# Order of the Hyena back transform, and operand loads of the RWKV scan issued one by one

## What is computed

```
def hyena_mixer(u, conv_w, conv_b, filt, skip):
    ...
    x0, x1, v = jnp.split(uc, 3, axis=-1)
    z = (v * x1).astype(jnp.float32)
    ...
    y = jnp.fft.irfft(jnp.fft.rfft(z, n=2 * L, axis=1) * jnp.fft.rfft(k2, axis=0)[None],
                      n=2 * L, axis=1)[:, :L]
    y = y + z * skip.astype(jnp.float32)
    return (x0.astype(jnp.float32) * y).astype(u.dtype)

def wkv7_scan(r, w, k, v, a, b, reverse):
    def step(S, inp):
        rt, wt, kt, vt, at, bt = inp
        sa = jnp.einsum('bhvk,bhk->bhv', S, at)
        S = S * wt[:, :, None, :] + sa[..., None] * bt[:, :, None, :] + vt[..., None] * kt[:, :, None, :]
        return S, jnp.einsum('bhvk,bhk->bhv', S, rt)
```

## Time and profile before

| | |
|---|---|
| median of 3 runs | 1851.04 us (1849.76 to 1853.55) |
| profiled execution | 1853.01 us, span of the trace 1851.2 us |
| DVE, ACT, POOL busy | 61%, 46%, 14% of the span |
| mean granted clock of PE | 0.967 |
| operand loads of the scan | 64 of 320 KB |

### The profile page before, as it was taken

How to read it: one execution, slowest core, us unless ns; L and a number is a source line. 1 busy time by engine, 2 the same in 40 slices (tenths; PEclk the granted TensorE clock), 3 DMA queues, 4 the chain that set the end, 5 groups by cost and what they waited for, 6 DMA issues and landing times. The chain is left out here.

```text
span 1851.2 us, 41734 instructions
## 1 busy us (share of the span) xinstructions
PE 1675.9 (91%) x17234; PEld 1269.7 (69%) x17234; DVE 1136.6 (61%) x1971; ACT 844.1 (46%) x1342; POOL 267.4 (14%) x337
## 2 busy tenths in 40 slices
PE   5999999998978889888887996999999999999995
PEld 4767777786745778777785885666666666666762
DVE  5558888746666444565456575556656655656754
ACT  4346666522322344444344111566556556656533
POOL 0020000002120433443340000000000000000003
PEclk9999999998989999999998996999999999999997
DMA  5224454433143111111103136689989989989927
GB/s 168 80 91 125 123 148 118 137 125 128 66 151 130 61 60 61 60 61 61 61 4 135 69 142 250 264 355 375 373 342 372 375 357 372 375 353 360 391 111 284
DMA packets 100356, 355.24 MB, mean 192 GB/s; under 512 B 16775, under 2 KB 56071, under 8 KB 85736
## 3 DMA queue, kind: packets, MB, share of 16 engines
q1 hardware_dynamic: 87528, 306.83, 44.5%
q0 software_dynamic: 8064, 29.36, 4.0%
q10 hardware_dynamic: 4608, 16.78, 2.2%
HBM read 294.75 MB, written 56.10 MB: 190 GB/s over the span
## 5 line engine op out<-in xcount | busy, mean ns | idle before, releaser
L2371 DVE TENSOR_TENSOR e_rl<-proj,e_rh 128x1024 fp32r<-128x1024 f32 x256 | 304.4, 1222 | 145.4 <-ACT e_rh L2307 144.4
L2307 ACT ACTIVATE e_rh<-proj 128x1024 fp32r<-128x1024 f32 x256 | 258.8, 1054 | 49.5 <-PE e_ph L51 30.0
L51 PE MATMUL e_ph<-e_rh,e_xh 128*128 128x512 f32 x512 | 220.7, 431 | 16.6 <-DVE e_rl L2371 14.0
L2288 PE MATMUL e_py<-mix,proj 128*128 128x512 f32 x512 | 225.0, 592 | 0.7 <-issue 0.7
L51 PE MATMUL e_ph<-e_rh,e_xl 128*128 128x512 f32 x512 | 201.6, 394 | 0.0
L51 PE MATMUL e_ph<-e_rl,e_xh 128*128 128x512 f32 x512 | 200.8, 392 | 0.0
L51 PE MATMUL a_b<-a_xh,a_wh 128*128 128x512 f32 x432 | 177.7, 411 | 5.7 <-DVE a_wl L587 3.2
L2288 PEld LDWEIGHTS e_py<-mix,proj 128*128 128x128 f32 x512 | 97.0, 190 | 110.7 <-issue 108.1
L51 PE MATMUL a_b<-a_xh,a_wl 128*128 128x512 f32 x432 | 169.7, 393 | 0.0
L51 PE MATMUL a_b<-a_xl,a_wh 128*128 128x512 f32 x432 | 169.6, 393 | 0.0
L51 PEld LDWEIGHTS e_ph<-e_rh,e_xh 128*128 128x128 f32 x512 | 97.4, 190 | 47.3 <-DVE e_rl L2371 19.7
(11 more groups left out here) (382 smaller groups left out, 3214.9 us busy)
## 6 DMA issues: line engine op xcount, KB each, us to landing
proj<-in_moe_w SPq DMA_DIRECT2D x64, 2048.0 KB, 14.2
mix<-in_moe_w SPq DMA_DIRECT2D x32, 2048.0 KB, 8.5
proj<-scan_operands SPq DMA_DIRECT2D x64, 320.0 KB, 4.2
expert_rows<-e_yo ACTq DMA_DIRECT2D x32, 512.0 KB, 11.1
scan_operands<-late SPq DMA_DIRECT2D x56, 256.0 KB, 2.6
proj<-in_w_in SPq DMA_DIRECT2D x27, 512.0 KB, 4.1
proj<-in_x SPq DMA_DIRECT2D x16, 512.0 KB, 6.4
expert_rows<-proj SPq DMA_DIRECT2D x1, 7680.0 KB, 21.5
```

The costliest lines, as they stand in the source:

```text
L51: m = e.matmul(out, lhs[a], rhs[b], start=first and n == 0, stop=last and n == 2)
L2288: m = e.matmul(py[h][:, :], at[:, k, :], w2[j][:, k, h * HALF:(h + 1) * HALF], start=(k == 0), stop=(k == KF - 1))
L2307: e.activation(rh[s % RING][:, :], piece(j, s), ACT.Copy).then_inc(high, 1)
L2371: e.tensor_tensor(rl[s % RING][:, :], piece(j, s), rh[s % RING][:, :].bitcast(F32), ALU.subtract).then_inc(low, 1)
```

## The change

In `mixers` the order of the 16 back pieces is taken from a table: outputs 0 and 1 for the double tiles 0 to 2 (six pieces), then double tile 3 for both, then outputs 2 and 3 as before. Piece 35 is now output 1 of double tile 0; double tile 3 comes first as piece 38. `outputs_of` follows the table. The product with x0 for channel tile 0 moves from the end of the block to the place behind `outputs_of(1)`.

In `rwkv_scan` SP waits after each operand DMA until it has landed, for the steps 2 to 15. The loads of steps 0 and 1 stay as they are.

```diff
                 def back(n):
-                    co, i = n // FH, n % FH
+                    co, i = BACK[n]
...
                     for co in range(2 * HY_C):
-                        if before < 8 * FH + 4 * co + 4 <= done:
+                        if before < 8 * FH + BACK.index((co, FH - 1)) + 1 <= done:
                             outputs_of(co)
+                        if co == 1 and before < 8 * FH + 2 * FH <= done:
+                            e.drain()
+                            e.tensor_tensor(S.mix[:, 0, :], zc[:, 0, :], x0[:, 0, :], ALU.mult)
...
                 e.drain()
-                for c in range(HY_C):
-                    e.tensor_tensor(S.mix[:, c, :], zc[:, c, :], x0[:, c, :], ALU.mult)
+                e.tensor_tensor(S.mix[:, 1, :], zc[:, 1, :], x0[:, 1, :], ALU.mult)
...
+BACK = ([(co, i) for co in range(2) for i in range(FH - 1)] + [(co, FH - 1) for co in range(2)]
+        + [(co, i) for co in range(2, 2 * HY_C) for i in range(FH)])
...
-def load_operands(e, S, n):
+def load_operands(e, S, n, paced=False):
...
             e.dma_start(operands(S, n % 2)[:, g, d, :, :], S.ops[p + g, d, t, :, :, :]).then_inc(S.op_in[n % 2], 16)
+            if paced:
+                e.wait_ge(S.op_in[n % 2], n // 2 * 64 + (2 * d + g + 1) * 16)
...
                     e.wait_ge(op_free, n - 1)
-                    load_operands(e, S, n)
+                    load_operands(e, S, n, paced=True)
```

## The result

The changed kernel takes 1833.07 us in the median of 6 runs (1828.82 to 1842.45), against 1850.4 for the kernel before (6 runs, 1846.13 to 1855.64). The ratio is 0.9906 with a 95% interval of 0.9886 to 0.9926: 17.4 us faster, give or take 3.7. The forecast was 1830.4 us, 20.6 faster.

A forecast was written before the change was run, and what follows sets the result against it. PE, busy 91% of the span, was taken to bound the kernel. From the 1851.04 us median, 8.6 us for the block (7.75 - 0.35 + 1.18) and 12 for paced loads gave 1830.4 us; 8-in-10 range 1820 to 1844.

The forecast's parts named there:

- The order of the pieces: Back pieces at piece 35: PE no longer waits for line 1049, round 12 opens at 553.13, gain 7.75 us.
- The outputs: Product moved to round 13: PE loses about 0.35 us in round 14, 1.18 us gained at the block's end.
- The cost of pacing: Scan: SP's waits cost nothing, unless one load alone takes above 5.7 us.
- The gain of pacing: Scan: shorter bursts delay PE's instruction fetches less, 12 us gained, with 0 and 25 us as ends.
- The ceiling: Scan: load bursts cost at most 17.9 us, 1.38 us in each of 13 steps against the step without loads.
- The share of two thirds: Scan: pacing recovers two thirds of 17.9 us, as a fetch waits 0.7 us on average instead of 2.5.
- The picture of PE's waits: Scan, 13 steps: PE's waits for instructions come down from 32.9 to some 12 us.
- Rival A: Scan: pacing gives nothing, the stops come from PE's own pace of use; 1842.4 us, chance 0.20.
- C: Round 12: POOL and DVE make PE wait as long there; block gives 0.8 us, total 1838.2 us, chance 0.06.
- D: Block and scan: C and Rival A together, or a change not doing what it says; 1850.2 us, chance 0.05.
- B: Scan: one late fetch starts a whole chain of stops, pacing gains 17.9 to 25 us; 1824.5 to 1817.4, chance 0.14.
- E: Scan: pacing stretches loading so three fetches per step are held up, 39 us more; 1881 us, chance 0.05.

The follow-up runs named there:

- pairs of loads: The changed kernel with SP waiting after every second operand load instead of every one: ratio 0.9919, median 1834.0 us.
- the block alone: The changed kernel with scan loads unpaced again, keeping the new piece order and moved product: 0.9952 of the kernel before; measured again, 0.9944.
- double loads: The kernel before with each scan step's four loads followed by four more of the same size into spare room: ratio 1.0109, 20.2 us slower.

## Why the prediction was right, step by step

**The order of the pieces.** Forecast 7.75 us, by laying the sequence of double tile 2 behind line 1049. The trace has round 12 at 552.57, 8.31 us before the 560.88 of the earlier trace rows, of which 0.58 had come up earlier: 7.73. From line 1049 to the next opening it is 4.54 us here as there. The clock stayed at 1.00, as said. The order alone, measured in two further traces, gives 7.74. This step was right in mechanism and size. (Three other profiles with the old order have 60.14 or 60.15 us for the block, where the kernel before has 59.77, so its gain is 8.6 to 9.0 us by the traces.)

**The outputs.** Forecast: DVE 0.4 us late in round 14, PE 0.35 us, and 1.18 us gained at the end. In the trace DVE's line 1078 starts at 574.34; 582.31 of the earlier trace rows less 8.31 would be 574.00, so it is 0.34 late. The piece behind the output transposes starts at 578.64 where 578.38 was due, 0.26 late. Moving the product is worth 0.87 us by the traces with and without it, where the forecast was 1.18 - 0.35 = 0.83. The block gives 8.60 us, the forecast sum; the first matmul was forecast at 591.3 and stands at 590.76, the difference being the 0.58 us from elsewhere.

**The cost of pacing.** None, as forecast. A load alone lands in 3.4 us in the median of the 56 paced ones, between the bounds of 2.8 and 4.2; five take longer, the longest 5.1 us, and none the 5.7 us at which the cover would break. (The 7.5 us of the row above is one of the eight unpaced loads of steps 0 and 1.) The four take 12.1 to 16.5 us, where 11.2 to 16.8 was forecast.

**The gain of pacing.** Forecast 12 us; the paced loads alone gave 12.0, and the two profiles differ by 10.9 in 13 steps. The ceiling by the earlier trace rows, 17.9 us, is near the 19.8 measured without loads. This was in part luck: it rests on the one step without a load, 22.76 us, and the same step takes 23.36 us in the kernel after, by which the ceiling would have been 10 us. The share of two thirds also came out (12.0 of 19.8 us is 0.61), but its working is not borne out: the packets of a single load spread over 2.0 us in the median, not 1.3, and pairs of loads, which by the same working should have given only 5 to 9 of the 12 us, cannot be told from single ones. The picture of PE's waits was wrong: I expected 32.9 us of them to come down to some 12, which is 21 us of waits for a gain of 12, and they came down to 25.9 (23.1 with the paced loads alone, 20.7 in the second profile of the kernel after). I had read them all as the work of the bursts, and 15.9 us are there with no loads at all. Rival A was wrong as a whole and right in that half., which I took as the delay itself, were weak evidence. Just ahead of that burst, from 811.7 to 817.9, the kernel before has 6.2 us with no DMA packet of any kind, so without an instruction packet although no load runs. The view of DMA there:

```profile
DMA packets 0, 0.00 MB, mean 0 GB/s; under 512 B 0, under 2 KB 0, under 8 KB 0
```

Only the counts of long gaps over 13 steps, with and without loads, show what a load does. That the number for the time was good rests on the step lengths with and without loads, not on the sum of the waits.

**The total.** 20.6 forecast, 17.4 and 15.4 measured in two comparisons. The parts measured alone give 20.9, so no term is plainly too large; but together they came out lower both times, by less than the intervals can settle. One candidate is seen in the traces. After the block the low clock lasts for a varying time. In the kernel before it lasts until 608:

```profile
600.00:608.00 8.00, 5.67 (x88) 5.09 (x88) 5.14 (x38) 2.06 (x7) 1.77 (x3) 0.50 0.01 3
608.00:612.00 4.00, 2.43 (x61) 2.01 (x62) 2.00 (x3) 2.16 (x4) 3.86 (x5) 1.00 0.00 0
```

In the kernel with the block alone the scan starts 8 us earlier, yet in its first profile the clock comes back at 608.6 only:

```profile
600.00:608.00 8.00, 6.43 (x109) 5.98 (x112) 2.85 (x5) 2.69 (x5) 7.19 (x7) 0.50 0.35 111
608.00:612.00 4.00, 2.88 (x104) 2.31 (x100) 0.76 (x2) 1.81 (x5) 0.00 (x0) 0.92 0.28 110
```

Its first step then takes 29.34 us, against 26.9 before and 26.5 in both profiles of the kernel after. In the second profile of the same code the clock is back after 6.8 us, and the step takes 26.61 us.

The fourteen profiles fall into two groups by this:

| clock back, behind the scan's first matmul | profiles | first step |
|---|---|---|
| 7.2 to 8.5 us | before and the three others with the old order; of the new order both of the kernel after, and the second of the block alone | 26.5 to 26.9 us (28.6 with double loads) |
| 16.1 to 17.4 us | the seven others, all of the new order | 29.3 to 29.6 us |

In the second group the block's gain of 8.6 us is cut to some 6. Both profiles of the kernel after are in the first group and are the fastest of their six runs, so the median runs may well be in the second; that would explain some 2.5 us of the shortfall, but the profiles do not show the other runs. In the prediction I looked at the clock round piece 35 and not at what the earlier start of the next block does to it.

**The rivals.** C (the stall moves) and D are out by the timeline and by the block alone. B (everything comes back) would have needed 17.9 us or more from the scan alone, and the interval of the paced loads ends at 16.1. E (three late fetches per step) is out: paced loads are faster, and long gaps between instruction packets became fewer, 12 against 16.

## What to carry to other kernels

Where a chain passes from one engine to another and back, look for an earlier round in the same trace that has the same instructions in the wanted order: the gain worked out from it was right here to 0.02 us. Where an engine waits for instructions while others' transfers run in bursts, compare many stretches with and without the transfers before adding up the waits, since part of the waits may be there without them (15.9 of 32.9 us here). When the profile gives no reason for a stop, look at how long before its end a packet of the instruction queue landed. A block that ends earlier starts the next one at another moment, and what depends on the moment, here the clock, belongs in the sum.

## What was unexpected of the hardware

The length of the low clock at the start of the scan is not set by the code: in two executions of the block alone it was 17.1 and 6.8 us. It was 10.2 us in the four profiles with the old order, 6.8 us in both of the kernel after, and 17.1 us in both of the order alone. The first step cost 2.4 to 3.1 us more where the clock came back late. With 3.66 us of PE's idle time filled with transposes it lasted 13.7 us, and it fell behind the next wait of PE, of 3.19 us.

PE's instruction supply suffers from transfers that have nothing to do with it. One set of operand loads per step, 17 MB in 13 steps, costs 20 us, of which 17 us are waits for instructions. In all 47 of these waits in the kernel before PE starts again 1.2 to 1.7 us after an instruction packet has ended.

Executions of one kernel differ by up to 5.6 us in the scan (304.77 and 310.40 us for the same code), and all medians here rest on that; parts of a change of a few us need several comparisons.
